# Last gate, branch and output projections of a DeltaNet/attention/MoE layer as three rounded passes

## What is computed

```python
h = rms_norm(x, g_norm1) * (1.0 + sc1) + sh1          # sc1, sh1, gt1, ... from c @ w_ada
proj = h @ w_in                                        # dn_qkv, dn_z, ..., gate_a, gate_b
o_a = gated_delta_rule(q_a, k_a, v_a, g, beta)
o_a = rms_norm(o_a, g_onorm) * silu(dn_z)
y_a = o_a.reshape(B, S, DN_W) @ w_o_delta              # (256 x 512) @ (512 x 1024)
o_b = forgetting_attention(q_b, k_b, v_b, log_f)
y_b = o_b.reshape(B, S, FOX_W) @ w_o_fox               # (256 x 512) @ (512 x 1024)
merged = sigmoid(gate_a) * y_a + sigmoid(gate_b) * y_b
x = x + gt1 * (merged @ w_out)                         # (256 x 1024) @ (1024 x 1024)
h2 = rms_norm(x, g_norm2) * (1.0 + sc2) + sh2
x = x + gt2 * moe_ffn(h2, ...)                         # 32 experts, top 4, gate/up 1024 x 2048, down 1024 x 1024
return rms_norm(x, g_final)
```

## Time and profile before

| | |
|---|---|
| median of 3 runs | 1219.63 us |
| lowest, highest | 1215.86, 1221.70 us |
| the profiled execution's own time | 1219.17 us |
| its span, mean granted TensorE clock | 1216.8 us, 0.981 |
| PE busy | 1128.8 us (93%) |
| DVE, ACT, POOL busy | 361.9, 185.3, 116.0 us |
| read from memory | 463.1 MB, 381 GB/s over the span |

### The profile page before, as it was taken

The page is one execution under the profiler, slowest core; times in us unless marked ns, Lnnn a source line. Parts: engine busy times, 40 slices in busy tenths (PEclk is TensorE's granted clock), DMA queues, the critical chain, the costliest instruction groups (busy, mean ns, idle before and its releaser), DMA issues.

```text
span 1216.8 us, 14754 instructions
## 1 busy us (share of the span) xinstructions
PE 1128.8 (93%) x6181; PEld 583.3 (48%) x6181; DVE 361.9 (30%) x690; ACT 185.3 (15%) x317; POOL 116.0 (10%) x50
## 2 busy tenths in 40 slices
PE   5998999999999999998989899899989999999897
PEld 2898899887443334333333333343324344333332
DVE  1677567352322121221221212122121223122112
ACT  2465444103100000000000000000000010000002
POOL 0775544020000000000000000000000000000000
PEclk9998999999999999999999899999989999999999
DMA  9987535498999999999999999999999999999995
GB/s 353 354 279 236 180 105 209 155 403 342 399 402 428 429 430 430 430 431 430 430 435 432 432 431 431 431 431 431 431 425 430 430 434 434 431 431 429 424 428 241
DMA packets 54513, 464.68 MB, mean 382 GB/s; under 512 B 7087, under 2 KB 29992, under 8 KB 33486
## 3 DMA queue, kind: packets, MB, share of 16 engines
q1 hardware_dynamic: 53644, 462.91, 91.9%
q10 hardware_dynamic: 786, 1.14, 0.3%
q0 software_dynamic: 48, 0.13, 0.0%
HBM read 463.13 MB, written 1.05 MB: 381 GB/s over the span
## 4 chain that ended last, share of the span: by engine, by line
PE 61%; DMA 32%; issue 2%; ACT 2%; POOL 1%; DVE 1%; SPq 0%; DVEq 0%; ACTq 0%
PE ps L511 59%; DMA ring<-in_w_down_dram 20%; DMA ring<-in_w_gate_up_dram 6%; DMA kept<-in_w_down_dram 3%; DMA ring<-in_w_ada_dram 2%; POOL w_lo L1857 1%; PE ps L979 1%; ACT kept L1330 1%; DMA ring<-in_w_in_dram 1%; ACT w_hi L1136 1%; PE ps L1011 0%; SPq L351 0%; DVE kept L1477 0%; PE ps L878 0%; SPq L389 0%
## 5 line engine op out<-in xcount | busy, mean ns | idle before, releaser
L511 PE MATMUL ps<-ring,kept 128*64 128x512 f32 (+2 forms) x2928 | 645.9, 601 | 31.4 <-DMA ring<-in_w_down_dram 20.4
L511 PEld LDWEIGHTS ps<-ring,kept 128*64 128x64 f32 (+2 forms) x2928 | 209.3, 139 | 442.0 <-issue 397.4
L511 PE MATMUL ps<-kept 128*128 128x128 f32 (+5 forms) x952 | 191.6, 419 | 7.7 <-ACT kept L1330 3.3
L511 PEld LDWEIGHTS ps<-kept 128*128 128x128 f32 (+2 forms) x952 | 106.3, 178 | 95.2 <-issue 82.8
L1759 DVE TENSOR_SCALAR kept<-ps 128x512 f32<-128x512 f32 x32 | 22.1, 692 | 379.1 <-PE ps L511 379.1
L1781 DVE TENSOR_TENSOR kept<-ps,kept 64x512 f32<-64x512 f32 x64 | 44.1, 689 | 298.1 <-PE ps L511 297.1
L1326 ACT ACTIVATE kept<-kept 128x512 f32<-128x512 f32 x32 | 20.2, 630 | 728.3 <-DVE kept L1759 728.3
L1857 POOL TENSOR_TENSOR w_lo<-ring,w_hi 128x1024 fp32r<-128x1024 f32 x38 | 101.8, 2698 | 97.0 <-ACT w_hi L1136 97.0
L511 PE MATMUL ps<-hT_hi,w_hi 128*128 128x256 f32 x272 | 78.7, 289 | 1.8 <-POOL w_lo L1857 1.8
L511 PE MATMUL ps<-hT_lo,w_hi 128*128 128x256 f32 x272 | 76.8, 282 | 0.0
L511 PE MATMUL ps<-hT_hi,w_lo 128*128 128x256 f32 x272 | 76.8, 282 | 0.0
(11 more groups left out here) (233 smaller groups left out, 553.0 us busy)
## 6 DMA issues: line engine op xcount, KB each, us to landing
ring<-in_w_gate_up_dram SPq DMA_DIRECT2D x54, 4096.0 KB, 27.9
ring<-in_w_down_dram SPq DMA_DIRECT2D x47, 2048.0 KB, 23.6
ring<-in_w_gate_up_dram SPq DMA_DIRECT2D x19, 2048.0 KB, 21.4
kept<-in_w_down_dram SPq DMA_DIRECT2D x16, 2048.0 KB, 25.1
ring<-in_w_ada_dram SPq DMA_DIRECT2D x24, 1024.0 KB, 7.3
ring<-in_w_in_dram SPq DMA_DIRECT2D x22, 1024.0 KB, 8.5
ring<-in_w_out_dram SPq DMA_DIRECT2D x4, 1024.0 KB, 13.2
ring<-in_w_o_fox_dram SPq DMA_DIRECT2D x2, 1024.0 KB, 6.0
```

Of the source, the lines that this page charges most:

```text
L511: return pe.matmul(dst, lhsT, rhs, start=start, stop=stop, skip_group_check=True)
```

## The change

Gates 6 and 7, both branch projections and the output projection become three rounded passes as well. 

- `SPLIT` gets 10 more units. ACT writes all their high halves; there are seven buffers now instead of three, the four new ones in the arena over masks, mixer data and inverse matrices that are no longer read. POOL writes the low halves of gates 6 and 7, of `w_o_fox` and of `w_o_delta`, and its bias work lies between the two units of `w_o_fox`. **DVE writes the low halves of `w_out`** (`out_lo`).
- The units of the branches and of the output are column blocks now (512 columns x 4 tiles, 256 columns x 8 tiles) instead of row blocks, so a transfer has rows of 2 KB and 1 KB instead of 4 KB.
- The moving side is split too: ACT rounds obT, oaT and merged (`obT_hi`, `oaT_hi`, `merged_hi`), DVE writes the low halves. obT's is written in the first chunk of the delta rule. oaT and merged are computed in place in zT and gates first.
- On PE fox columns 6 and 7 both stand behind the transposes of o. The low-x-high pass of a column pair comes last, behind its own wait. The matmul of `lpart` (a constant of the router) and what DVE does for it move from the second `w_o_delta` pair behind the second `w_out` pair.
- `hT_whole` is gone. ACT copies all of `h2tok` behind the root, since `merged_lo` lies in its place.
- The fetches of the first two experts are issued in another order, as the buffers allow.
- Several small semaphores share a name now, with a count in place of a name each.

```diff
-        SPLIT += [("gates", u) for u in range(6)]
-        HI_BUF = [n % 2 for n in range(BEFORE_GATES)] + [0, 1, 1, 1, 2, 2]
+        SPLIT += [("gates", u) for u in range(8)]
+        AFTER_GATES = len(SPLIT)
+        SPLIT += [("wo_fox", u) for u in range(2)] + [("wo_delta", u) for u in range(2)]
+        SPLIT += [("w_out", u) for u in range(4)]
+        HI_BUF = [n % 2 for n in range(BEFORE_GATES)] + [0, 1, 1, 1, 2, 2, 3, 4] + [5, 6, 3, 4] * 2
...
-        UNITS += [("w_out", u, rows_unit(w_out, 256 * u, 2)) for u in range(4)]
+        UNITS += [("w_out", u, columns_unit(w_out, 256 * u, 256)) for u in range(4)]
...
+            def split_products(dst, name, u, ms, nk, mov_hi, mov_lo, hi_wait, lo_wait, early=()):
+                n = SPLIT_AT[(name, u)]
+                hi = hi_buf_r(n)
+                lo = unit_r(UNIT_AT[(name, u)]).rearrange("p (k n) -> p k n", k=split_rows(n))
...
+                for ks in (early, [k for k in range(nk) if k not in early]):
+                    for j, c in enumerate(cols):
+                        half = c.start // (UNIT // nk // 2)
+                        if name == "w_out":
+                            pe.wait_ge(S("out_lo"), 2 * u + 1 + half)
+                        else:
+                            pe.wait_ge(S("split_lo"), 2 * n + 1 + half)
+                        for k in ks:
+                            hi_wait(k)
+                            for stat in (hi, lo):
+                                last = mm(dst(j), stat[:, k, c], mov_hi[:, k, :], not begun, False)
+                                begun = True
+                lo_wait()
+                for j, c in enumerate(cols):
+                    for k in range(nk):
+                        last = mm(dst(j), hi[:, k, c], mov_lo[:, k, :], False, k == nk - 1)
...
-                    for t in range(TT):
-                        last = take_h2tok(t, 0)
-                    last.then_inc(S("h2tok_taken"), 1)
...
-            for t in range(TT):
-                last = take_h2tok(t, 1)
-            last.then_inc(S("h2tok_taken"), 1)
+            for b in range(2):
+                for t in range(TT):
+                    last = take_h2tok(t, b)
+                last.then_inc(S("h2tok_taken"), 1)
...
             sp.wait_ge(S("oT_ps"), 1)
-            for j in range(2):
-                load_dn(0, 0, j)
+            load_dn(0, 0, 1)
+            sp.wait_ge(S("oaT_ready"), 2)
+            load_gu(1, 1, 0, 2, 2)
             sp.wait_ge(S("yb_ps"), 4)
             load_gu(0, 0, 1, 2, 2)
-            load_gu(1, 1, 1, 0, 2)
             sp.wait_ge(S("ya_ps"), 4)
             load_gu(0, 0, 0, 0, 2)
+            load_gu(1, 1, 1, 0, 2)
+            sp.wait_ge(S("merged_ready"), 4)
+            load_gu(1, 1, 0, 0, 2)
+            sp.wait_ge(S("out_ps"), 2)
+            load_gu(0, 0, 0, 2, 2)
+            load_dn(0, 0, 0)
+            sp.wait_ge(S("out_ps"), 4)
+            load_gu(0, 0, 1, 0, 2)
             load_gu(1, 1, 1, 2, 2)
```

More of the change, by code:

```diff
@@ L1274, in _ @@
                              accum_out=oss[:, t, h:h + 1])
+                if t == 0:
+                    split_unit("wo_delta", 1)
             link(last)
@@ L1869, in _ @@
                     S("bias_split"), 1)
+            pool.wait_ge(S("bias_split"), 5)
+            for n in range(SPLIT_AT[("wo_fox", 1)], SPLIT_AT[("w_out", 0)]):
+                split_lo(n)
             pool.wait_ge(S("logits_ps"), 1)
```

305 lines of the change are left out of this document (181 added, 124 removed).

## The result

The changed kernel takes **1208.07 us** (median; undisturbed runs 1207.93 to 1208.15) against 1218.08 of the kernel before beside it: ratio 0.9921, 95% interval 0.9904 to 0.9938. One run of it took 2310 us and is not counted. Forecast: 1210.2, range 1205.5 to 1215.5. The sign, the size and the moment of the fetches behind the last output pair came out as forecast; several of the terms that add up to it did not.

The account below looks back on a forecast made before the run. The end was taken as the DMA engines' last pause plus remaining bytes at 430 GB/s. PE savings of 13.7 us plus 0.3 less 5.0 of new waits gave 9.0: 1219.2 - 9.0 = 1210.2 us, range 1205.5 to 1215.5.

Parts of the forecast that it names:

- What bounds the kernel: Weight transfers: the end is when the DMA engines stop pausing, plus the bytes left at 430 GB/s.
- The most that the transfers can give, 11.3 us: Expert weight fetches: without any pause the next two start at 287 us, capping the gain whatever PE gains.
- Gates, 3.3 us: Late gates on PE: 32 products, each 0.103 us shorter as three rounded passes.
- Branches, 5.4: Branch projections on PE: 64 products, each 0.084 us shorter as three rounded passes, 5.4 us.
- Output, 5.0: Output projection on PE: 64 products, each 0.079 us shorter as three rounded passes, 5.0 us.
- The new waits, 5.0: PE from o's transposes to lpart: added waits on VectorE and GpSimd summing to 5.0 us.
- the walk: All queues followed through 202 to 297 us, VectorE and GpSimd excluding each other; old order within 0.4 us of the trace.
- Net 9.0, fetches at 287.5: Behind the last output pair: the last slots' fetches issued at about 287.5 instead of 296.5 us.
- a sign of failure: DMA engines: a pause opening between 245 and 285 us would show the forecast wrong.
- The transfers are the limit: PE's waits overlap less, fetches issue before 285.5 us, DMA engines run through: -11.3 us, 1207.9 us; chance 0.18.
- GpSimd late: Six halves after the bias work take 3.5 us each; PE waits 4 to 5 us more: 1214.5 us; chance 0.15.
- Rule against trace: VectorE and GpSimd with two SBUF inputs wait for each other; without exclusion the gain would be 12.5, cut to 11.3 us.

Follow-up runs that it names:

- after_again: The changed kernel profiled a second time, unedited; 1208.18 us, with a first gather of 5.44 us.
- both edits: Changed kernel with VectorE's two A2 instructions moved behind the first output pair and w_out's high-halves-by-low-merged pass left out; 1203.97 us against 1208.66.
- Experiment 7: Changed kernel with only the two branch projections put back to float32; 1210.13 us, ratio 0.9941 to the kernel before.
- experiment 6: Changed kernel with only the output projection put back to float32; 1214.09 us, ratio 0.9985 to the kernel before.
- A2 late: Changed kernel with VectorE's two 8-column A2 instructions moved behind the first output pair; 1208.99 and 1208.51 us against 1208.18 and 1208.66.
- experiment 5: Changed kernel with w_out's eight low halves written by GpSimd again instead of VectorE; 1214.68 us, ratio 0.9990 to the kernel before.

## Why the prediction was right, and where not

- **What bounds the kernel: right, with one thing left out.** "Whatever moves the end of the output projections and the start of the first expert together moves the end of the kernel by as much" holds within 1.4 us over thirteen profiles once the gather is allowed for. In the pair with the same long gather (after_again and before) the fetches come 7.8 us earlier and the end 7.8 to 8.3, with both edits 6.2 more and 6.5 more. The chain from the last output projection to the first gather "stays" in order but not in length: the gather takes 3.81 or 5.44 us by the granted clock, and the ends differ by 2.4 us with it, 1.6 of which are there already at the first slot that an expert frees. The forecast had no term for this.
- **The most that the transfers can give, 11.3 us: too low.** Both edits at once took 14.2 us off the median (1218.19 to 1203.97), with the fetches in the order of the changed kernel.
- **Gates, 3.3 us: too high.** A half takes 212.63 - 209.57 = 3.06 us from start to start where it took 3.65, so 0.59 x 4 = 2.4. This is the mis-sized term: 24 passes at the pitch of the earlier trace rows are 2.83 us, and the start of a lone group of 24, 0.23 us more, is not in that pitch.
- **Branches, 5.4: about right by itself, nearly nothing after what it cost.** A fox pair gained 0.6, a w_o_delta pair 3.53 - 2.88 = 0.65 at full clock, about 5 in all. The wait for oaT and the clock behind it took 3.9 back. Experiment 7 puts the net at 0.5.
- **Output, 5.0: about right.** 4.5 by experiment 6, and no wait against it in the changed kernel.
- **The new waits, 5.0: a sum not far off (3.9 measured), from the wrong places.** That it is so near is luck. Forecast 1.7 at the third w_o_delta pair, 1.5 at the first output pair, 0.3 at w_out's second unit, 0.9 at lpart: none of them is in the trace. Forecast 0.6 up to the first w_o_delta pair: it was 2.3, with 1.6 of clock behind it, for which there was no term. The step that failed is the walk's treatment of two VectorE instructions in a row. I had the earlier trace rows, where the first of two waits 2.26 us and the second passes, because GpSimd had no two-input work directly behind. Here six halves stand back to back, and each instruction pays one. Once PE was 3.9 us late, VectorE had the time to finish all that the other four terms were about; without that delay (A2 late) two of them appear, at 0.7 and 0.4 us.
- **Net 9.0, fetches at 287.5: 7.8.** The profile's 287.52 matches only because that run came to the mark 1.1 us earlier, which is luck. The terms as measured: 2.4 + 5.0 + 4.5 + 0.3 - 2.3 - 1.6 = 8.3.
- **The time.** 7.8 us on PE's path, and about 10 in the median (0.9921 of 1218.08 is 9.6). The short gather, worth 2.4 us, was found in two of three profiles of the changed kernel and in neither of the kernel before, which is about the difference; whether the change brings the short gather about or these five profiles fell so by chance is open. The forecast of 9.0 lies between the two numbers for no reason of its own.
- **What the profile after should show.** Right: pitch 0.118, GpSimd halves of up to 4.4 us (15.57 us for four at 209.62), first expert matmul at 300.04 against "near 301.5", 430 GB/s afterwards. Wrong: a pause between 245 and 285 us did open (share 0.66, 164 GB/s from 262 to 264 us), which I had named as a sign of failure, and the 2 us hole near 288 us did not. The forecast of the time held in spite of that sign; what the pause cost by itself no run separates from the wait ahead of it.
- **Rivals.** "The transfers are the limit" has the nearest time, 1207.9, but not by its mechanism: it wanted the fetches issued before 285.5 us and the DMA engines running through, and they came at 287.5 with a pause at 262. Both edits together still gained 4.7 us more. "GpSimd late" did not occur in the changed kernel: no wait for w_lo above 0.3 us. With w_out's halves put back on GpSimd it gives 1214.7, close to the 1214.5 of that rival, though through the merges and not through a late half.
- **Rule against trace.** VectorE's small instruction took 0.17 us alone and 1.98 to 2.42 beside a half (experiment 7). By the Trainium skill, "SBUF — State Buffer", section "SBUF: two separate sides", whoever comes first holds the shared ports for a whole instruction; the trace agrees, twice in a row. The warning in "Perfetto Trace Analysis", section "Optimizing Scalar/DVE Operations", that moving work between the two engines may not help did not come true here: the halves moved onto VectorE brought the fetches 4.6 us forward (experiment 5), because GpSimd then had no two-input work while the merges ran.

## What to carry to other kernels

When transfers fill the rest of a kernel, find the last pause and what ends it; a lead of 1.5 MB ahead of a pause that stayed was gone behind it here. Before two ends are compared, see whether the stretches that both kernels share ran at the same granted clock: here a gather of 3.81 or 5.44 us went with ends 2.4 us apart, which looked like an effect of the edits. Price each VectorE instruction that has two SBUF inputs and stands amid a row of GpSimd subtractions at one whole GpSimd instruction, however small it is, and every such instruction again (two in a row took 1.98 and 2.42 us here); move the tiny ones to where GpSimd is idle. Compare profiles from a mark in unchanged work, since the moment of reaching it scatters by as much as the effect.

## What the runs showed of the hardware

- The exclusion depends on where the inputs are: amid GpSimd's halves L1476 and L1681, with an input in PSUM, took 0.16 and 0.68 us, while L1724, with both in SBUF, took 1.98, and in experiment 5 L1753 took 2.54 instead of 0.69.
- An idle stretch of 2.3 us on TensorE was followed by a granted clock of 0.66 to 0.81 at 250 to 255 us in all seven profiles with that wait, and of 1.00 in the four of the changed kernels without it. It cost 1.6 us, two thirds of the wait again.
- The 32 small products of the first gather took 3.81 us at a granted clock of 1.00 in four profiles and 5.28 to 5.44 us where a part of them ran at the lower level, in nine. One and the same kernel shows both, with the same waits ahead of it.
- At a DMA share of 1 the same stretch of 45 us carried 398, 411 and 431 GB/s in three kernels with the same list of fetches. In the kernels with three passes it was 396 to 398 GB/s with the long gather and 409 to 411 with the short one. No run here says why a full share is worth more or less.
